# An RWKV-7 chunk inverse on one NeuronCore: its last level becomes a fourth turn of TensorE's loop, with bonus, scores and part of the vector work moved

## What is computed

```python
def step(S, inp):                      # 8 heads of 64 channels, 256 tokens
    r_t, w_t, k_t, v_t, a_t, b_t = inp
    sa = jnp.einsum('bhvk,bhk->bhv', S, a_t)
    S = S * w_t[:, :, None, :] + sa[..., None] * b_t[:, :, None, :] + v_t[..., None] * k_t[:, :, None, :]
    return S, jnp.einsum('bhvk,bhk->bhv', S, r_t)
...
y = ((y - mean) * lax.rsqrt(var + GN_EPS)).reshape(B, T, D_RWKV) * lnx_w + lnx_b
bonus = jnp.sum(r * k * r_k, axis=-1, keepdims=True) * v
return (y + bonus.reshape(B, T, D_RWKV)) * g
...
y = jnp.concatenate([y_rwkv, y_nsa], axis=-1)
h = h + y @ w_out[i]
```

## Time and profile before

| | |
|---|---|
| median of 3 runs | 721.77 us (721.59 to 721.95) |
| the profiled execution | 720.93 us |
| its span (first to last instruction) | 718.9 us |
| PE, DVE, ACT, POOL busy | 97%, 73%, 58%, 2% of the span |
| HBM read | 112.01 MB, 157 GB/s over the span |

### The profile page before, as it was taken

One profiled execution on the slowest core, in us unless ns is written; L12 is line 12 of the kernel. 1 busy time (PEld: TensorE's weight loads), 2 busy tenths in 40 slices (PEclk: granted clock), 3 DMA queues, 4 the chain that ended last, 5 costly groups with the idle time before them and its releaser, 6 DMA issues.

```text
span 718.9 us, 15450 instructions
## 1 busy us (share of the span) xinstructions
PE 696.6 (97%) x6106; PEld 606.0 (84%) x6106; DVE 522.8 (73%) x957; ACT 416.4 (58%) x738; POOL 15.8 (2%) x23
## 2 busy tenths in 40 slices
PE   6999999999999999998999999998999999999996
PEld 5877778988888888888898888787988888888885
DVE  4574647678989996447677896776678999985456
ACT  5565555575756665436887765444575666665332
POOL 0000000020000000000100000000110000000000
PEclk9999999999999999999999999999999999999999
DMA  6542322536665555552443351411335555545531
GB/s 228 209 143 78 118 96 81 173 122 234 250 216 210 204 204 176 185 199 92 170 175 119 118 176 67 172 62 61 118 131 196 201 198 206 180 175 193 210 124 58
DMA packets 16735, 113.73 MB, mean 158 GB/s; under 512 B 2000, under 2 KB 2128, under 8 KB 3632
## 3 DMA queue, kind: packets, MB, share of 16 engines
q1 hardware_dynamic: 15984, 109.22, 42.8%
q0 software_dynamic: 704, 3.85, 1.6%
HBM read 112.01 MB, written 1.05 MB: 157 GB/s over the span
## 4 chain that ended last, share of the span: by engine, by line
PE 85%; DVE 6%; ACT 4%; issue 2%; DMA 2%; DVEq 0%; SPq 0%; ACTq 0%
PE ps L622 22%; PE ps L624 11%; PE ps L684 9%; PE ps L597 8%; PE ps L599 7%; PE ps L598 7%; PE ps L686 5%; PE ps L1019 2%; PE ps L1006 2%; ACT w_hi L1552 1%; DVE w_lo L2037 1%; DMA ring<-in_weights 1%; PE ps L1087 1%; DMA vec<-in_vecs 1%; DVE acts L2239 1%
## 5 line engine op out<-in xcount | busy, mean ns | idle before, releaser
L2037 DVE TENSOR_TENSOR w_lo<-ring,w_hi 128x1024 fp32r<-128x1024 f32 x193 | 235.4, 1221 | 97.6 <-ACT w_hi L1552 96.3
L1552 ACT ACTIVATE w_hi<-ring 128x1024 fp32r<-128x1024 f32 x193 | 203.3, 1055 | 114.9 <-PE ps L686 51.5
L622 PE MATMUL ps<-acts,w_hi 128*128 128x512 f32 x704 | 246.6, 393 | 0.8 <-ACT act_in L1705 0.7
L624 PE MATMUL ps<-acts,w_lo 128*128 128x256 f32 x704 | 197.4, 280 | 0.0
L622 PEld LDWEIGHTS ps<-acts,w_hi 128*128 128x128 f32 x704 | 132.2, 188 | 31.6 <-DVE acts L2239 1.9
L597 PE MATMUL ps<-acts,w_hi 128*128 128x256 f32 (+1 forms) x456 | 136.3, 299 | 1.8 <-DVE acts L2622 0.7
L624 PEld LDWEIGHTS ps<-acts,w_lo 128*128 128x128 f32 x704 | 132.3, 188 | 0.1
L599 PE MATMUL ps<-acts,w_lo 128*128 128x256 f32 (+1 forms) x456 | 129.5, 284 | 0.0
L598 PE MATMUL ps<-acts,w_hi 128*128 128x256 f32 (+1 forms) x456 | 129.2, 283 | 0.0
L597 PEld LDWEIGHTS ps<-acts,w_hi 128*128 128x128 f32 x456 | 85.8, 188 | 13.2 <-issue 9.1
L684 PE MATMUL ps<-hid,w_hi 128*128 (+1 forms) x272 | 94.4, 391 | 0.0
(11 more groups left out here) (389 smaller groups left out, 937.2 us busy)
## 6 DMA issues: line engine op xcount, KB each, us to landing
ring<-in_weights SPq DMA_DIRECT2D x101, 1024.0 KB, 4.8
res<-in_xT SPq DMA_DIRECT2D x2, 544.0 KB, 4.2
ring<-in_weights SPq DMA_DIRECT2D x2, 512.0 KB, 5.8
cst<-in_consts POOLq DMA_DIRECT2D x1, 1024.0 KB, 5.1
out_features<-yT SPq DMA_DIRECT2D x4, 256.0 KB, 2.2
cst<-in_consts POOLq DMA_DIRECT2D x1, 945.5 KB, 4.8
vec<-in_vecs POOLq DMA_DIRECT2D x1, 677.0 KB, 4.2
cst<-in_consts POOLq DMA_DIRECT2D x1, 656.0 KB, 9.9
```

The lines of the kernel that those rows point to most:

```text
L622: pe.matmul(ps[:, bank, :].rearrange("p (x t) -> p x t", x=2), w_hi[:, slot, k, :], acts[:, :, at, 0:SEQ], start=(k == 0), stop=(k == KT - ...
L624: return pe.matmul(ps[:, bank, 0:SEQ], w_lo[:, slot, k, :], act_hi[:, at, 0:SEQ], start=False, stop=(k == KT - 1), skip_group_check=True)
L1552: act.activation(w_hi[:, t % SLOTS].rearrange("p k c -> p (k c)"), ring[:, b % RING, half].rearrange("p k c -> p (k c)"), ACT.Copy)\
L2037: dve.tensor_tensor(w_lo[:, t % SLOTS].rearrange("p k c -> p (k c)"), ring[:, b % RING, half].rearrange("p k c -> p (k c)"), w_hi[:, t % S ...
```

## The change

Six parts.

1. Query tiles of the first block's projection (six of 21: `QS + QF`) leave out the 16 meta tokens: `first_token(t)`; PE's three products and DVE's copy run over 256 columns and not 272.
2. `products(c)` leaves out four of its eight L1183 products; `masked(c)` takes these triangles from the wider product's bank with a mask operation of its own.
3. PE's loop has four turns and not three, in another order: joined(0), grow_xt(1) of the level before, grow_xi(0), joined(1), grow_xt(0), grow_xi(1). DVE fills in that order.
4. `value_tokens` stand ahead of the loop, `cmp_compressed`, `cmp_scores` and bonus(1) behind it; bonus(1) in bank 6, behind sa_of(0).
5. POOL does the end of the compressor's softmax and `gate_b` (bias and gate), which DVE did; ACT's weighting of the gates (L1966 before) stands behind the attended rounding.
6. ACT's and DVE's splits of output tiles 2 and 3 stand later; `outputs((0,))` behind state_after(2).

```diff
+def first_token(t):
+    return META if t in QS + QF else 0
...
+            pool.wait_ge(S("xt_grown_1"), LEVELS - 1)
+            for g in range(KVH):
+                ins = pool.tensor_tensor(den_c[:, :, g * GQA:(g + 1) * GQA], den_c[:, :, g * GQA:(g + 1) * GQA],
+                                         gv[:, :, g, :, 0], ALU.mult)
+            step(ins)
+            step(pool.tensor_tensor(den_c, den_c, C("cmp_any").unsqueeze(2).to_broadcast([P, 2, NQH]), ALU.mult))
+            pool.tensor_tensor(flat_s, flat_s, flat_d.unsqueeze(2).to_broadcast([P, 2 * NQH, CMP_PAD]), ALU.mult)\
+                .then_inc(S("cmp_vector"), 1)
+
+            pool.wait_ge(S("bonus_kept"), 2)
+            for j in range(PAIRS):
+                ins = pool.tensor_scalar(gate_b[:, j, :], gate_b[:, j, :], V("lnx_b", j), None, ALU.add)
+            step(ins)
+            pool.tensor_tensor(gate_b[:, :, :], gate_b[:, :, :], gate_w[:, :, :], ALU.mult).then_inc(S("bonus_gated"), 1)
...
-                tile_products(ps[:, t % 2, 0:CTX], (T_IN1 + t) % SLOTS, CTX, "norm1" if t == 0 else None, between)\
+                c0 = first_token(t)
+                tile_products(ps[:, t % 2, c0:CTX], (T_IN1 + t) % SLOTS, CTX, "norm1" if t == 0 else None, between, c0)\
...
-                for j in range(PAIRS):
-                    at = P + j * HD
+                for y in range(PAIRS // 2):
+
+                    at = P + y * HD
                     for h, hs in halves():
-                        pe.matmul(ps[hs, b, at:at + HD], bb[hs, j, ts], ar[hs, 0, j, ts], start=True, stop=True,
-                                  skip_group_check=True)
+                        pe.matmul(ps[hs, b, at:at + HD], bb[hs, 2 * y + 1, ts], ar[hs, 0, 2 * y + 1, ts], start=True,
+                                  stop=True, skip_group_check=True)
...
+            pe.wait_ge(S("bonus_kept"), 1)
+            value_tokens(TOKEN_BANKS, 0)
             grow_xt(0)
-            bonus(1)
+            pe.wait_ge(S("tokens_kept"), 1)
+            value_tokens(TOKEN_BANKS, 1)
             hidden(3)
             pe.wait_ge(S("join_kept_1"), 1)
             grow_xi(1)
-            grow_xt(1)
             cmp_folded()
...
+            with pe.Fori(0, LEVELS - 2) as i:
+                pe.wait_ge(S("xi_grown_0"), grown[0])
+                pe.reg_add(grown[0], grown[0], 1)
+                joined(0)
+                grow_xt(1)
+                pe.wait_ge(S("xt_grown_0"), i + 1)
+                pe.wait_ge(S("join_kept_0"), kept[0])
+                pe.reg_add(kept[0], kept[0], 1)
+                grow_xi(0)
+                pe.wait_ge(S("xi_grown_1"), grown[1])
+                pe.reg_add(grown[1], grown[1], 1)
+                joined(1)
+                grow_xt(0)
+                pe.wait_ge(S("xt_grown_1"), i + 1)
+                pe.wait_ge(S("join_kept_1"), kept[1])
+                pe.reg_add(kept[1], kept[1], 1)
+                grow_xi(1)
+
             pe.wait_ge(S("join_kept_1"), LEVELS - 1)
             pe.wait_ge(S("xt_grown_1"), LAST)
             grow_xt(1)
-            pe.wait_ge(S("tokens_kept"), 2)
+            cmp_compressed()
+
+            key_values(JOIN_BANKS[0], 0)
             pe.wait_ge(S("rk_ready"), 2)
             turn_tokens(JOIN_BANKS[1], bb, 0)
+            pe.wait_ge(S("cmp_scalar"), 3)
+            cmp_scores(2, 0)
             pe.wait_ge(S("tokens_kept"), 3)
             turn_tokens(JOIN_BANKS[0], key_raw, 0)
-            pe.wait_ge(S("xt_grown_1"), LEVELS - 1)
-            pe.wait_ge(S("cmp_vector"), 3)
-            key_values(TOKEN_BANKS, 1)
+            cmp_scores(2, 1)
...
             sa_of(0)
             state_ahead(0)
+            pe.wait_ge(S("xt_grown_1"), LEVELS - 1)
+            bonus(1)
+            pe.wait_ge(S("cmp_vector"), 3)
+            key_values(TOKEN_BANKS, 1)
+            state_after(0)
+            cmp_turn()
             pe.wait_ge(S("tokens_kept"), 6)
             turn_tokens(TOKEN_BANKS, bb, 1)
-            cmp_turn()
-            state_after(0)
-            pe.wait_ge(S("tokens_kept"), 7)
-            turn_tokens(TOKEN_BANKS, key_raw, 1)
             from_state(1)
             state_ahead(1)
             sa_of(1)
-            pe.wait_ge(S("tokens_kept"), 8)
-            outputs((0,))
+            pe.wait_ge(S("tokens_kept"), 7)
+            turn_tokens(TOKEN_BANKS, key_raw, 1)
             state_after(1)
             from_state(2)
-            cmp_values(6)
+            pe.wait_ge(S("tokens_kept"), 8)
             state_ahead(2)
             sa_of(2)
+            pe.wait_ge(S("bonus_kept"), 2)
+            cmp_values(6)
+            state_after(2)
+            outputs((0,))
             outputs((1,))
-            state_after(2)
             from_state(3)
```

More of the change, by code:

```diff
@@ L1323, in _ @@
             grow_xi(1)
-            grow_xt(1)
             cmp_folded()
-            grown, kept = [pe.alloc_register(f"grown_{m}") for m in range(2)], [pe.alloc_register(f"kept_{m}") for m in range(2)]
+            pe.wait_ge(S("tokens_kept"), 2)
+            grown, kept = [[pe.alloc_register(f"{n}_{m}") for m in range(2)] for n in ("grown", "kept")]
             for m in range(2):
@@ L1331, in _ @@
                 pe.reg_mov(kept[m], 2)
-            with pe.Fori(0, LEVELS - 3) as i:
-                for m in range(2):
-                    pe.wait_ge(S(f"xi_grown_{m}"), grown[m])
-                    pe.reg_add(grown[m], grown[m], 1)
-                    joined(m)
-                for m in range(2):
-                    pe.wait_ge(S(f"xt_grown_{m}"), i + 1)
-                    pe.wait_ge(S(f"join_kept_{m}"), kept[m])
-                    pe.reg_add(kept[m], kept[m], 1)
-                    grow_xi(m)
-                    grow_xt(m)
-            pe.wait_ge(S("xi_grown_0"), LAST)
-            joined(0)
-            cmp_compressed()
-            pe.wait_ge(S("xi_grown_1"), LAST)
-            joined(1)
-            pe.wait_ge(S("join_kept_0"), LEVELS - 1)
-            pe.wait_ge(S("xt_grown_0"), LAST)
-            grow_xt(0)
-            value_tokens(JOIN_BANKS[0], 0)
-            pe.wait_ge(S("cmp_scalar"), 3)
-            pe.wait_ge(S("bonus_kept"), 2)
-            cmp_scores(2, 0)
-            cmp_scores(2, 1)
-            pe.wait_ge(S("join_kept_1"), LEVELS - 1)
-            value_tokens(JOIN_BANKS[1], 1)
-            key_values(JOIN_BANKS[0], 0)
+            with pe.Fori(0, LEVELS - 2) as i:
[15 more added lines that the diff above has]
+                grow_xi(1)
             pe.wait_ge(S("join_kept_1"), LEVELS - 1)
@@ L1963, in _ @@
             split_hi(T_OUT2)
-            act.wait_ge(S("bonus_gated"), 1)
-            for j in range(PAIRS):
-                ins = act.activation(gate_w[:, j, :], gate_w[:, j, :], ACT.Copy, scale=V("lnx_w", j))
-            ins.then_inc(S("gates_weighted"), 1)
             keep_join(0, 4)
@@ L1995, in _ @@
                     .then_inc(S("act_rounded"), 1)
+            act.wait_ge(S("bonus_gated"), 1)
+            for j in range(PAIRS):
+                ins = act.activation(gate_w[:, j, :], gate_w[:, j, :], ACT.Copy, scale=V("lnx_w", j))
+            ins.then_inc(S("gates_weighted"), 1)
             def output_squares(cp):
@@ L2014, in _ @@
             output_squares(0)
+            split_hi(T_OUT2 + 3)
             output_root(0)
@@ L2538, in _ @@
             fill_xt(0, 1)
-            bonus_kept(1)
             fill_xi(1, 1)
-            fill_xt(1, 1)
             def fill(level):
-                for m in range(2):
-                    fill_xi(m, level)
-                    fill_xt(m, level)
+                fill_xt(1, level - 1)
+                fill_xi(0, level)
+                fill_xt(0, level)
+                fill_xi(1, level)
             flat_h = hid_f.rearrange("p x c -> p (x c)")
@@ L2560, in _ @@
             dve.tensor_tensor(flat_h, flat_h, gel, ALU.mult).then_inc(S("cmp_vector"), 1)
-            dve.wait_ge(S("bonus_kept"), 2)
-            for j in range(PAIRS):
-                ins = dve.scalar_tensor_tensor(gate_b[:, j, :], gate_b[:, j, :], V("lnx_b", j), gate_w[:, j, :],
-                                               ALU.add, ALU.mult)
-            ins.then_inc(S("bonus_gated"), 1)
             fill(3)
@@ L2587, in _ @@
                 .then_inc(S("cmp_vector"), 1)
-            fill_xt(1, 5)
+            fill_xt(0, 5)
+            dve.wait_ge(S("cmp_scalar"), 4)
+            step(dve.tensor_reduce(flat_d, flat_s, AX.X, ALU.add))
+            dve.reciprocal(flat_d, flat_d)
             own = C("cmp_own").rearrange("p (a c) -> p a c", a=GQA)
             dve.tensor_tensor(vown, own, vown_src.unsqueeze(1).to_broadcast([P, GQA, P]), ALU.mult)
+            fill_xt(1, 5)
             def keep_sa(c):
```

63 lines of the change are left out of this document (29 added, 34 removed).

## The result

| | before | the change |
|---|---|---|
| median of 5 runs each | 721.59 us | 729.61 us (727.52 to 731.38) |
| the profiled execution | 720.93 us | 727.52 us |
| its span | 718.9 us | 725.7 us |

The ratio is 1.0108, 95% interval 1.0095 to 1.0122: slower by 7.8 us. The forecast was 723.6, its range up to 725.8. The sign was right; 6.0 us are missing from the forecast.

A forecast was written before the change was run, and what follows sets the result against it. PE, busy 97% of the span, was taken as the bound. First block -1.0, later start of outputs((2, 3)) +1.35 and clock +1.5 gave +1.85 on 720.93, 722.8; with 0.84 for the median, 723.6 us, range 720.8 to 725.8.

The forecast's parts named there:

- First block, products, ahead of the loop: Up to the loop: savings of 1.0, 0.7 and 0.7 us; loop start at 457.1, the first block's 1.0 not counted.
- The loop: PE's loop: a turn takes 4.2 us against 4.54 before, a half turn 1.6 + 0.5; four turns end at 473.9.
- Rival C: Loop: the 0.2 us handover wait does not show, a turn takes 3.8; sum +0.25, 722.0 us; chance 0.15.
- Behind the loop, to the scores' end: PE's blocks from the loop's end at 473.9 through both halves of the scores, ending at 479.5.
- The wait behind the scores: PE waits 3.4 us behind the scores for DVE's and ACT's softmax steps and token copies; sa_of(0) at 482.9.
- sa_of(0) to from_state(1): From 482.9 to 487.5, with 0.4 us added for unnamed PE stops and a wait ahead of bonus(1); before, from_state(1) at 486.52.
- The clock: At least one fall of PE to half clock in or behind the wait after the scores; cost 0 to 3 us, 1.5 taken.
- Rivals A and D: A: clock falls inside PE's wait or not at all, 722.1 us, chance 0.22. D: that plus Rival C, 720.5, chance 0.08.
- POOL's gates: POOL's wide product 2.6 us, additions 0.5 each; done at 495.7, just ahead of DVE's rest_attended at 495.8: no cost.
- rival B: POOL's wide product blocks DVE's rest_attended and PE's first out_part: 0 to 3.7 us; 725.5 us in mid-bounds; chance 0.15.
- Sum: Whole kernel: -1.0 first block, +1.35 up to outputs((2, 3)), +1.5 clock, giving +1.85 us and a forecast of 723.6.

The follow-up runs named there:

- x3: The changed kernel with three turns in PE's loop and the fourth written out behind it, same instructions and order; 1.0090, 728.75 us.
- x67: The changed kernel with the edits of both x6 and x7: no wait behind the scores, weights one turn earlier; 1.0022, 722.72 us.
- x7: The changed kernel with the splits of output tiles 0 and 1 one loop turn earlier, so the next weights load sooner; 1.0076, 725.94 us.
- x6: The changed kernel with ACT's copies of tokens 4 and 5 and DVE's level-5 fills ahead of the softmax steps; 1.0049, 724.84 us.
- x467: x67 with bias and gate of gate_b on DVE and off POOL; 1.0006, 721.63 us.
- x4: The changed kernel with bias and gate of gate_b on DVE and off POOL; 1.0112, 729.61 us.
- x9: x2e with the load of output tiles 2 and 3 held until the loop's first copy of joined(0); 0.9954, 718.02 us; again 0.9965, 717.72 us.
- x2: The kernel before with parts 1 and 2 of the change alone; 0.9996, 720.82 us.
- x2e: x2 with output tiles 0 and 1 split a turn earlier, DVE's bias and gate and ACT's gate weighting moved; 0.9979, 719.47 us.
- x1: The kernel before with part 1 of the change alone; 0.9988, 720.97 us.
- bhe: x9 without parts 1 and 2: the kernel before with only the earlier splits and the held load; 1.0002, 721.21 us; again 1.0002, 721.38 us.

## Why the prediction was wrong, step by step

- **First block, products, ahead of the loop:** the loop began at 456.11, where the sum had 457.1 less the first block's 1.0. Tile by tile the query tiles are 1.0 us shorter, as foretold. That the start fits to 0.1 is in part luck: at 439 the change was 1.4 us ahead of before, 0.4 more than the sum, since executions differ that much in their first 60 us; and from there to the loop it gained 1.0 and not 1.4, because of the stop of 0.4 ahead of the loop.
- **The loop:** starts of joined(0) at 456.11, 460.70, 465.05, 469.39, end at 473.52: 4.35 a turn, not 4.2. The half turn is as foretold: in the second turn grow_xi(0) starts 1.58 behind joined(0), joined(1) 0.49 behind that. What was left out is the turn's end, 0.71 from grow_xi(1) to the next joined(0) where a block takes 0.49. DVE's fills for it were done 1.3 us before, and in x3's written-out turn this 0.2 is not there (468.80 to 469.29). It makes 0.6 us in all. Rival C is out; its bound of 3.8 should have been 3.7 by its own terms.
- **Behind the loop, to the scores' end: the step that failed.** The sum had 5.6 us of PE work, 473.9 to 479.5. In x67, where nothing stands in the way, the same work takes 6.1 (473.39 to 479.5); in the change 10.0 (473.52 to 483.5). The 3.9 between are the stop of 1.9, and 2.0 because all behind it ran at half clock (0.50 from 479.8, as PE went on, to 490.1). With the stop gone, in x7, the whole way from the loop's end to sa_of(0) took 9.5, where the sum had 9.0. The step had PE's work and PE's waits for other engines in it, and for the supply of instructions nothing but the 0.4 of the next sentence. The sentence "Twice before PE stood some 0.2 to 0.3 us for no reason that the trace names; I add 0.4" is where it could have been seen: the trace marks three such places, 0.9 us together, as issue, and the packets stand in its DMA view. I had taken a shortage for noise, and the queue of weights was in no step although SP's load moved with the splits.
- **The wait behind the scores:** 3.4 foretold, 3.11 measured, ended by ACT's copy as foretold. x6 puts its price, with the clock in it, at 4.3 us.
- **sa_of(0) to from_state(1):** 5.2, not 4.6, the most of it at half clock; PE did not wait ahead of bonus(1).
- **The clock:** the sum took 1.5 out of 0 to 3. The half clock lasted 10.2 us and cost about 3 (2.0 ahead of the wait, 0.9 at bonus(1), 2.07 against 1.12). So a half clock came, as foretold, but most of its price fell ahead of the wait and not behind it. Rivals A and D needed the full clock back by 484; it came at 490.1.
- **POOL's gates:** the wide product 2.36 (taken 2.6), but the additions 0.9 each (taken 0.5), at the upper end of the bounds. The Trainium skill's 4.5 us (GPSIMD Engine Reference, Elementwise) is for an addition of two tensors, not for a product as the prediction has it; half of it, an estimate of 2.2 to 2.3, fits this product all the same. rest_attended was ready 4.6 behind bonus_kept, as foretold (4.7); POOL needed 6.1. So rival B's mechanism came on top of the forecast and did not replace it: 1.1 us by PE's wait (1.75 against 0.66), and as much by x467 against x67. The Trainium skill's rule on exclusive access (SBUF — State Buffer, Who interferes with whom) agrees with the 1842 ns of the one instruction.
- **Sum.** outputs((2, 3)) stood at 507.48; the prediction, with the first block's 1.0 and the clock's 1.5 in it, had it at 502.5. The 5.0 are: the loop 0.6, blocks 0.5, the stop 1.9, half clock ahead of the wait 2.0, sa_of(0) to from_state(1) 0.6, from there on 1.2 (POOL's 1.1 in it), less 0.3 for the shorter wait and the 1.5 for the clock that were in the sum. The median is another 2.1 above the profiled execution (before 0.7), and why is not shown, since this kernel has one profile; the stop of 2.3 us ahead of the loop, found in the profiled executions of x4, x6 and x7, is of that size.

In ratios, from the change back to before: 7.8 us slower; the wait behind the scores off, 3.5; the weights moved as well, 1.6; POOL's gates as well, 0.4. So mended, the new order with parts 1 and 2 in it ends where before does; the old order with the same parts and its weights moved (x9) ends 3 us earlier.

## What to carry to other kernels

Where a queue holds long runs of short instructions, count them: PE's come 256 to a packet, and a packet that is wanted while a block of weights moves came only near the block's end. Look for "issue" in the waits and for lone packets in the DMA view before costing an edit there, and place bulk loads inside loops, from the second turn on, where no packet moved; the first turn can still need one (x2 and x2e stopped in it). When work is taken out ahead of such a place, it may come back there unless the packets are freed too (x2 against x9). And two rivals can both come: a range that takes them one at a time is too narrow.

## What the runs showed that was not expected

- A stop for instructions of up to 2.6 us, nearly as long as the largest wait between engines in this stretch (3.1). In the 27 such stops between 440 and 490 of all the profiles PE goes on 2.2 to 2.8 us behind the packet's start, in 24 of them 2.2 to 2.5. The packet does not always wait for the last of the weights: x3's starts 0.6 us before it, one of x1 in the loop's first turn (461.4) 1.7 us.
- Behind one in the loop's first turn no packet moved until its end (none from 459.2 to 477.4 in the change), though its body is 192 records, more than one packet. Behind it the next comes 0.7 to 1.4 us after the loop's end where no weights are in the way (before, x3, x67).
- The half clock does not belong to the scores alone. Behind them it was 3.4 us before, 0 in x1, x2 and x2e, 3.4 in both executions of x9, 6.8 and 3.4 in the two of bhe, 3.4 in x67 (from 484.8), 10.2 in the change; 7 us of it followed the stop ahead of the loop in x4, x6 and x7. In before it cost nothing that x1 could win back, since the packet held PE anyway; in x9 it was there and the kernel was the fastest. What it costs by itself was not tried.
- POOL's addition of a scalar to 128x256 took 916 ns. That is more than its product of two tensors of that size behind the scores (L608, 623 ns) and than a quarter of the 128x1024 one (590 ns). The 1.04 us of the earlier trace rows, which the prediction took as POOL's price, is for the sums of squares and was too high for both products.
